# Recurrent heads of a hybrid layer: pairs of different 128-token chunks through carried 128x128 states instead of blocks of a dense 512x512 weight matrix

## The reference, cut to what matters

```python
def hgrn2_chunk_scan(q, k, v, g):
    """Chunkwise S_t = diag(exp g_t) S_{t-1} + k_t v_t^T, o_t = S_t^T q_t.
    q,k,g: (B,S,H,K), v: (B,S,H,V) float32, g = log forget gate. Returns (B,S,H,V)."""
...
    def step(state, inp):
        qc, kc, vc, gc = inp
        b = jnp.cumsum(gc, axis=2)
        diff = b[:, :, :, None, :] - b[:, :, None, :, :]
        decay = jnp.exp(jnp.where(tri[:, :, None], diff, -jnp.inf))
        att = jnp.einsum('bhtk,bhsk,bhtsk->bhts', qc, kc, decay)
        o = (jnp.einsum('bhts,bhsv->bhtv', att, vc)
             + jnp.einsum('bhtk,bhkv->bhtv', qc * jnp.exp(b), state))
        b_last = b[:, :, -1:, :]
        state = (jnp.exp(b_last[:, :, 0, :])[..., None] * state
                 + jnp.einsum('bhsk,bhsv->bhkv', kc * jnp.exp(b_last - b), vc))
        return state, o
```

## Time and profile before

| what | value |
|---|---|
| median of three runs | 3098.46 us (3096.57 to 3101.62) |
| profiled execution, its span | 3093.4 us |
| median less span (what lies around the span) | 5.1 us |
| TensorE busy | 2997.9 us, 97% of the span |
| weight loads busy | 2355.2 us, 76% |
| VectorE busy | 1750.6 us, 57% |
| ScalarE busy | 1000.6 us, 32% |
| GpSimd busy | 1976.8 us, 64% |

### The profile page before, as it was taken

How to read it: one execution, slowest core, us unless ns; L and a number is a source line. 1 busy time by engine, 2 the same in 40 slices (tenths; PEclk the granted TensorE clock), 3 DMA queues, 4 the chain that set the end, 5 groups by cost and what they waited for, 6 DMA issues and landing times.

```text
span 3093.4 us, 39590 instructions
## 1 busy us (share of the span) xinstructions
PE 2997.9 (97%) x15236; PEld 2355.2 (76%) x15236; DVE 1750.6 (57%) x2350; ACT 1000.6 (32%) x1712; POOL 1976.8 (64%) x1860
## 2 busy tenths in 40 slices
PE   8999999999999999999999999999999999899997
PEld 6887777788778878777877777777777777687686
DVE  7745887751374569777217443334788778801412
ACT  6243223330233331334103232233544454411422
POOL 6665676577676656756757655555567777566364
PEclk9999999999999999999999999999999999999998
DMA  5322222233223222222432222222212222232122
GB/s 210 110 102 103 82 93 84 82 142 123 99 106 109 102 86 90 97 82 75 172 109 97 84 86 70 83 72 77 79 69 83 73 80 81 93 133 98 66 89 89
DMA packets 59340, 298.68 MB, mean 97 GB/s; under 512 B 6512, under 2 KB 7408, under 8 KB 29200
## 3 DMA queue, kind: packets, MB, share of 16 engines
q1 hardware_dynamic: 36960, 251.67, 23.1%
q10 hardware_dynamic: 22192, 44.48, 4.2%
HBM read 274.04 MB, written 16.84 MB: 94 GB/s over the span
## 4 chain that ended last, share of the span: by engine, by line
PE 74%; DVE 16%; ACT 4%; POOL 3%; issue 2%; DMA 1%; ACTq 1%; DVEq 0%; POOLq 0%
PE bank L433 65%; POOL w_lo L2595 2%; DVE rec_ex L2432 1%; DVE rec_cum L2297 1%; PE bank L777 1%; POOL w_hi L2593 1%; ACT att_sc L1322 1%; PE bank L786 1%; PE bank L794 1%; DMA w_raw<-in_wall 1%; DVE newton L1796 1%; DVE newton L1798 1%; DVE bank L1899 1%; DVE att_sc L2173 1%; PE bank L966 1%
## 5 line engine op out<-in xcount | busy, mean ns | idle before, releaser
L433 PE MATMUL bank<-h_hi,w_lo 128*128 128x512 f32 x3712 | 1501.6, 405 | 24.7 <-POOL w_lo L2595 14.8
L433 PE MATMUL bank<-h_hi,w_hi 128*128 128x512 f32 x3712 | 1453.0, 391 | 0.0
L433 PE MATMUL bank<-h_lo,w_hi 128*128 128x512 f32 x3712 | 1451.5, 391 | 0.0
L2593 POOL TENSOR_SCALAR w_hi<-w_raw 128x512 fp32r<-128x512 f32 x928 | 705.3, 760 | 1004.0 <-PE bank L433 913.0
L2595 POOL TENSOR_TENSOR w_lo<-w_raw,w_hi 128x512 fp32r<-128x512 f32 x928 | 1294.0, 1394 | 77.4
L433 PEld LDWEIGHTS bank<-h_hi,w_lo 128*128 128x128 f32 x3712 | 700.6, 189 | 230.4 <-issue 52.2
L433 PEld LDWEIGHTS bank<-h_hi,w_hi 128*128 128x128 f32 x3712 | 700.1, 189 | 150.9
L433 PEld LDWEIGHTS bank<-h_lo,w_hi 128*128 128x128 f32 x3712 | 701.7, 189 | 146.2 <-issue 10.5
L1034 ACT ACTIVATE raw<-bank 128x512 f32<-128x512 f32 x148 | 88.5, 598 | 403.9 <-PE bank L433 366.3
L2098 DVE SCALAR_TENSOR_TENSOR bank<-cfm_up,par,bank 128x512 f32<-128x512 f32 x232 | 175.4, 756 | 8.3
L1805 DVE TENSOR_TENSOR sumsq<-sumsq,bank 128x512 f32<-128x512 f32 x80 | 55.0, 688 | 178.8 <-ACT bank L1718 144.7
(11 more groups left out here) (370 smaller groups left out, 2690.8 us busy)
## 6 DMA issues: line engine op xcount, KB each, us to landing
w_raw<-in_wall SPq DMA_DIRECT2D x230, 1024.0 KB, 4.9
x_scratch<-xT ACTq DMA_DIRECT2D x12, 1024.0 KB, 5.0
xT<-x_scratch ACTq DMA_DIRECT2D x12, 1024.0 KB, 8.9
ssd_abc<-acs_scratch ACTq DMA_DIRECT2D x16, 512.0 KB, 3.8
first_xin<-in_x SPq DMA_DIRECT2D x4, 1024.0 KB, 11.2
out<-last_z SPq DMA_DIRECT2D x4, 1024.0 KB, 4.1
w_raw<-in_wall SPq DMA_DIRECT2D x8, 256.0 KB, 10.2
att_tq<-att_uq ACTq DMA_DIRECT2D x32, 64.0 KB
```

What stands on the lines that cost most here:

```text
L433: mm = t.matmul(bank[BANK[u]][:, :], w[:, CS16[k]], h[:, k, :], start=(k == 0 and w is m.w_lo[b]), stop=(k == KT - 1 and w is m.w_hi[b] an ...
L2593: g.tensor_scalar(m.w_hi[b][:, part], m.w_raw[b][:, part], 1.0, 1.0, ALU.mult, ALU.mult).then_inc(*s.hi.inc(u, n))
```

## The change

Only chunks and their own tokens stay in A: `am` becomes 128x4x128, the diagonal blocks alone, and `combine` four matmuls of 128x128. Everything between different chunks goes through states of 128x128 (key width by value width), three for each direction, one for each chunk from which something flows on:

- `keys(j)` on TensorE, in the place of `far(j)`: six transposes of the decayed keys into banks 4 and 5; ScalarE copies them out (`keys`, two copies of 128x384).
- `states(j)` after level 2: six matmuls of 128x128, keys times values, into the same banks.
- `carried(j)` on VectorE, between its levels 3 and 4: two copies and four multiply-adds of 128x128, which carry each state to the next chunk.
- `far(j)` after level 4: six matmuls of 128x128, states times decayed queries `fq`, into bank 6; `combine` then adds to that bank.

VectorE makes the two decayed keys first and the two decayed queries second (into new tiles `fq`); `far_small` is gone; `gather` is one copy of 128x512 from bank 3 after level 1, and stands before `decays(j, 5)`. Head 7 has the same in the same places. The diff, with hunks left out that only repeat this for head 7 or remove a call:

```diff
@@ -52,6 +52,7 @@
 LEVELS = (16, 8, 4, 2, 1, 0)
+FAR_CHUNKS = ((0, 1, 2), (3, 2, 1))
 TWO_PI = 2.0 * math.pi
@@ -369,9 +370,8 @@
         self.lev = t("lev", [P, NLEV])
-        weights = t("weights", [P, NC * (T + P)])
-        self.am = [weights[:, c * T:(c + 1) * T] for c in range(NC)]
-        self.diag = weights[:, :].rearrange("p (c n) -> p c n", n=T + P)
+        self.am, self.keys = t("am", [P, NC, P]), t("keys", [P, 6, P])
+        self.fq = [t(f"fq{d}") for d in range(2)]
         assert m.at >= m.band.end
@@ -826,36 +826,48 @@
             t.wait_ge(*act.at("evac", UNIT["hv", 2, j]))
-            if j:
-                t.wait_ge(*act.at("oT", 3, j - 1))
             for c in range(NC):
...
+        def keys(j):
+            t.wait_ge(*dve.at("fk", j))
+            for d, chunks_of in enumerate(FAR_CHUNKS):
+                for n, c in enumerate(chunks_of):
+                    mm = t.transpose(bank[4 + d][:, CS[n]], q.lk[d][:, CS[c]], m.ident)
+            mm.then_inc(*pe.inc("keys", j))
+
+        def states(j):
+            t.wait_ge(*act.at("keys", j))
+            t.wait_ge(*act.at("vtok", 3, j))
+            for d, chunks_of in enumerate(FAR_CHUNKS):
+                for n, c in enumerate(chunks_of):
+                    mm = t.matmul(bank[4 + d][:, CS[n]], q.keys[:, 3 * d + n, :], q.vtok[:, c, :], start=True, stop=True)
+            mm.then_inc(*pe.inc("states", 3, j))
+
         def far(j):
-            Q = lambda d, c: q.lq[d][:, CS[c]]
-            K = lambda d, c: q.lk[d][:, CS[c]]
-            q2 = q.small
-            pairs = [(0, 1, 0, Q(0, 1)), (0, 2, 0, q2[:, 0, :]), (0, 3, 0, q2[:, 2, :]), (1, 2, 0, Q(0, 2)),
-                     (1, 3, 0, q2[:, 1, :]), (2, 3, 0, Q(0, 3)), (1, 0, 1, Q(1, 0)), (2, 1, 1, Q(1, 1)),
-                     (2, 0, 1, q2[:, 3, :]), (3, 2, 1, Q(1, 2)), (3, 1, 1, q2[:, 4, :]), (3, 0, 1, q2[:, 5, :])]
-            t.wait_ge(*dve.at("fk", j))
-            t.wait_ge(*act.at("q2", j))
-            for src, dst, d, rhs in pairs:
-                mm = t.matmul(bank[3 + src][:, CS[dst]], K(d, src), rhs, start=True, stop=True)
+            t.wait_ge(*dve.at("st", 3, j))
+            if j:
+                t.wait_ge(*act.at("oT", 3, j - 1))
+            for d, chunks_of in enumerate(FAR_CHUNKS):
+                for n, c in enumerate(chunks_of):
+                    to = c + 1 - 2 * d
+                    mm = t.matmul(bank[6][:, CS[to]], q.small[:, 3 * d + n, :], q.fq[d][:, CS[to]], start=(d == 0 and n == 0), stop=False)
             mm.then_inc(*pe.inc("far", j))
...
             t.wait_ge(*dve.at("lev", j, n))
+            if n == 0 and j:
+                t.wait_ge(*act.at("am", j - 1))
             if n == 2:
...
                     for x in range(0, P, 2 * h):
-                        mm = t.matmul(bank[3 + c][x:x + 2 * h, o + x:o + x + 2 * h], q.lk[b][:, o + x:o + x + 2 * h],
+                        mm = t.matmul(bank[3][x:x + 2 * h, o + x:o + x + 2 * h], q.lk[b][:, o + x:o + x + 2 * h],
                                       qq[:, o + x:o + x + 2 * h], start=True, stop=True)
@@ -867,7 +879,7 @@
             for c in range(NC):
-                mm = t.matmul(bank[2][:, :], q.vtok[:, c, :], q.am[c], start=(c == 0), stop=(c == NC - 1))
+                mm = t.matmul(bank[6][:, CS[c]], q.vtok[:, c, :], q.am[:, c, :], start=False, stop=(c == NC - 1))
             mm.then_inc(*pe.inc("o", 3, j))
@@ -885,7 +897,7 @@
                 quarters(us, 0, 4)
-            far(j)
+            keys(j)
             quarters(us, *((4, 5) if j == 0 else (0, 2)))
@@ -895,10 +907,12 @@
             level(j, 2)
+            states(j)
             quarters(us, 6, 8)
...
             level(j, 4)
+            far(j)
             quarters(us, 9, 11)
@@ -1549,14 +1565,14 @@
             a.wait_ge(*act.now())
-            a.activation(chunks(q.ex[1][:, 0, :]), f[:, :, inc], ACT.Exp).then_inc(*act.inc("far0", j))
-            a.wait_ge(*act.now())
             a.activation(q.gx[:, 1, :], q.gx[:, 1, :], ACT.Exp).then_inc(*act.inc("far1", j))
...
             a.wait_ge(*act.now())
+            a.activation(chunks(q.ex[1][:, 1, :]), g[:, :, exc], ACT.Exp).then_inc(*act.inc("far3", j))
+            a.wait_ge(*act.now())
+            a.activation(chunks(q.ex[1][:, 0, :]), f[:, :, inc], ACT.Exp).then_inc(*act.inc("far0", j))
+            a.wait_ge(*act.now())
             a.activation(q.gx[:, 0, :], q.gx[:, 0, :], ACT.Exp).then_inc(*act.inc("far2", j))
-            a.wait_ge(*act.now())
-            a.activation(chunks(q.ex[1][:, 1, :]), g[:, :, exc], ACT.Exp).then_inc(*act.inc("far3", j))
             a.wait_ge(*act.now())
@@ -1564,17 +1580,14 @@
                 a.wait_ge(*act.now())
-                a.activation(q.diag[x:x + 32, :, x:x + 32], q.near[x:x + 32, :].rearrange("p (c n) -> p c n", n=32),
+                a.activation(q.am[x:x + 32, :, x:x + 32], q.near[x:x + 32, :].rearrange("p (c n) -> p c n", n=32),
                              ACT.Copy).then_inc(*act.inc("near", j))
...
-        def far_small(j):
-            Q = lambda d, c: q.lq[d][:, CS[c]]
-            w = [q.g2[:, d, c:c + 1] for d in range(2) for c in range(2)]
-            a.wait_ge(*dve.at("fq", j))
-            for n, (src, f1) in enumerate(((Q(0, 2), w[0]), (Q(0, 3), w[1]), (q.small[:, 1, :], w[0]), (Q(1, 0), w[2]),
-                                           (Q(1, 1), w[3]), (q.small[:, 3, :], w[3]))):
+        def keys(j):
+            a.wait_ge(*pe.at("keys", j))
+            for d in range(2):
                 a.wait_ge(*act.now())
-                a.activation(q.small[:, n, :], src, ACT.Copy, scale=f1).then_inc(*act.inc("q2", j))
+                a.activation(q.keys[:, 3 * d:3 * d + 3, :], chunks(bank[4 + d][:, 0:3 * P]), ACT.Copy).then_inc(*act.inc("keys", j))
...
@@ -1585,15 +1598,14 @@
         def gather(j):
-            a.wait_ge(*pe.at("level", j, 7))
-            for c in range(NC):
-                a.wait_ge(*act.now())
-                a.activation(q.am[c], bank[3 + c][:, :], ACT.Copy).then_inc(*act.inc("am", j))
+            a.wait_ge(*pe.at("level", j, 1))
+            a.wait_ge(*act.now())
+            a.activation(q.am[:, :, :], chunks(bank[3][:, :]), ACT.Copy).then_inc(*act.inc("am", j))
...
             a.wait_ge(*act.now())
-            a.activation(m.y[:, 8 + j, :], bank[2][:, :], ACT.Copy).then_inc(*act.inc("oT", 3, j))
+            a.activation(m.y[:, 8 + j, :], bank[6][:, :], ACT.Copy).then_inc(*act.inc("oT", 3, j))
             if j:
@@ -1625,6 +1637,7 @@
             evac(u1, m.raw[1])
+            gather(j)
             decays(j, 5)
@@ -1634,19 +1647,19 @@
                 rstd_exp(j - 1)
-            gather(j)
             far(j + 1)
             near(j)
-            far_small(j + 1)
             decays(j + 1, 0)
...
         output(6)
+        keys(7)
         decays(7, 1)
...
         decays(7, 3)
+        gather(7)
         a.wait_ge(*pe.at("read", 2, 0))
@@ -2415,10 +2427,12 @@
             kd = q.kd[j % 2]
-            for dst, x, y, name, done in ((q.lq[0], q.ex[1][:, 0, :], q.qs[:, :], "far0", "fq"),
-                                          (q.lq[1], q.gx[:, 0, :], q.qs[:, :], "far2", "fq"),
-                                          (q.lk[0], q.gx[:, 1, :], kd[:, 0, :], "far1", "fk"),
-                                          (q.lk[1], q.ex[1][:, 1, :], kd[:, 1, :], "far3", "fk")):
+            if j:
+                v.wait_ge(*pe.at("far", j - 1))
+            for dst, x, y, name, done in ((q.lk[0], q.gx[:, 1, :], kd[:, 0, :], "far1", "fk"),
+                                          (q.lk[1], q.ex[1][:, 1, :], kd[:, 1, :], "far3", "fk"),
+                                          (q.fq[0], q.ex[1][:, 0, :], q.qs[:, :], "far0", "fq"),
+                                          (q.fq[1], q.gx[:, 0, :], q.qs[:, :], "far2", "fq")):
                 v.wait_ge(*act.at(name, j))
@@ -2435,7 +2449,7 @@
                 decays(j, n + 1)
-            v.wait_ge(*(pe.at("level", j, n - 2) if n >= 2 else pe.at("far", j)))
+            v.wait_ge(*(pe.at("level", j, n - 2) if n >= 2 else pe.at("keys", j)))
             if h:
@@ -2447,6 +2461,19 @@
                 v.tensor_tensor(q.lk[b][:, :], kd[:, 0, :], kd[:, 1, :], ALU.add).then_inc(*dve.inc("lev", j, n))
+
+        def carried(j):
+            v.wait_ge(*pe.at("states", 3, j))
+            v.wait_ge(*act.at("far4", j))
+            for d in range(2):
+                v.wait_ge(*dve.now())
+                v.tensor_copy(q.small[:, 3 * d, :], bank[4 + d][:, 0:P]).then_inc(*dve.inc())
+            for n in range(1, 3):
+                for d in range(2):
+                    c = FAR_CHUNKS[d][n]
+                    v.wait_ge(*dve.now())
+                    v.scalar_tensor_tensor(q.small[:, 3 * d + n, :], q.small[:, 3 * d + n - 1, :], q.g2[:, d, c - 1:c], bank[4 + d][:, CS[n]],
+                                           ALU.mult, ALU.add).then_inc(*dve.inc("st", 3, j))
...
@@ -2490,6 +2517,7 @@
             level(j, 3)
+            carried(j)
```

(7 more changed lines are left out.)

## The result

The changed kernel takes 3122.36 us (median; 3121.19 to 3124.26), the kernel before 3099.05 us on the same chip: ratio 1.0077, interval 1.0065 to 1.0089. It is slower; the forecast was 3122. Its profiled execution takes 3122.63 us, with a span of 3121.3; that of the kernel before has a span of 3093.4.

What follows compares the result with a forecast made beforehand. VectorE and ScalarE were taken to set the stretch before each level 0, TensorE the one after. 18.2 - 4.5 + 8.5 + 1.8 = +24.0 us on the span of 3093.4, plus 5.1, gave 3122 us; range 3107 to 3131.

Steps and rivals of the forecast that it cites:

- B: Stretch from the end of unit hq to the next level 0; VectorE and ScalarE set it, staying at 34.65 us.
- A: Stretch from level 0 to the end of hq, set by TensorE; grows 2.60 us in heads 0 to 6, +18.2.
- Head 0 really gains 4.5 of B: From head 0 to head 1 VectorE has no finish to do, so TensorE's saved work shortens the time: -4.5 us.
- The clock, 5 x 1.7: TensorE's granted clock falls after the 5.05 us pauses before level 0 of heads 2 to 6: +8.5 us.
- `carried` 1.9 us, hidden, 1.6 us of slack: Six VectorE operations between levels 3 and 4 take 1.9 us, ready 1.6 us before TensorE's level 4: no cost.
- The tail, +1.8: In head 7 VectorE is late, so its added 1.9 us push the end back: +1.8 us, bounds -0.8 and +2.
- The 5.1 us: Time between the profiled span and the median, added to the forecast span of 3117.4 to give 3122.5.
- TensorE is the bound: Rival: 1.90 us off every head, 8 x 1.9 = 15, time 3083, if B falls below 30.1; chance 0.08.
- The clock does not fall: Rival: no fall of TensorE's clock behind the pauses, 15.5 us slower in place of 24.0, time 3114; chance 0.10.
- the second rival: B shortens in part, as VectorE's operation times depend on GpSimd; 2.6 to 4 us less per head, 3093 to 3105; chance 0.08.

Runs made afterwards that it cites:

- run 2: Changed kernel with ScalarE's evacuation of unit hv ahead of the decays instead of behind them; 3119.31 us, ratio 1.0078.
- run 1: Changed kernel with VectorE's finish of the head before last put behind level 0 instead of before it; 3107.37 us, ratio 1.0036.
- run 11: Changed kernel with hv's evacuation first and finish's three root-refining VectorE operations left out in heads 0 to 5, for measuring only; 3094.21 us, ratio 0.9996.
- run 8: Changed kernel with hv's evacuation first, plus 18 unused filler matmuls ahead of level 0 in heads 2 to 6; 3115.47 us, ratio 1.0058.
- run 7: Changed kernel with states and far moved behind level 7 and quarter 13, carried into VectorE's gap before the logarithms; 3104.45 us, ratio 1.0023.
- run 3: Changed kernel with both moves: VectorE's finish behind level 0 and hv's evacuation ahead of the decays; 3106.54 us, ratio 1.0033.
- run 9: Changed kernel with finish in VectorE's gap, hv's evacuation first, three root-refining operations omitted in heads 0 to 5, for measuring only; 3085.01 us, ratio 0.9969.
- run 5: Changed kernel with VectorE's finish in its gap while waiting for ScalarE's logarithms, and hv's evacuation first; 3098.40 us, ratio 0.9999.

## Why the prediction was right

**Its mechanism is right. That the total is so close is in part luck: two of its terms missed by almost 4 us each, in opposite directions.**

- *B is VectorE's and stays*: right, 34.6 us, and the pause is 4.97 us in run 2, where it stands in one piece, against 5.05. Runs 1 and 11 show it by shortening B through VectorE alone, run 8 by giving TensorE more to do there at no cost.
- *A grows by 2.60*: right, 2.65 to 2.70 (the heads without a fall in A, 70.2 and 70.3 against 67.5 and 67.65); run 7 takes it back.
- *Head 0 really gains 4.5 of B*: wrong. It gained 2.4 (31.66 against 34.07), and with 4.4 more in A the head got 2.0 longer where -1.9 was forecast. The step that failed is that only VectorE's operands and TensorE's own work end this B. ScalarE's evacuation of hv was a third candidate. Before, it was hidden behind the six microseconds of `combine` and `far` that were taken away. Runs 2 and 11 show it: with the evacuation first this B is 29.5, and the 4.5 are there.
- *The clock, 5 x 1.7*: a fall follows the pauses in five heads, but it cost 5.0 in place of 8.5. The size of one is right (1.65 us in the three that fell in A, 1.6 in run 1, 1.4 by run 8). The count was off: the same ScalarE wait cut the pause in two, and two falls went into B, where they are hidden. A fall of 10.24 us in head 0 (3.41 before, and 3.41 in run 2) cost 2.4 us that were not counted (A of 32.6 against 30.2 in run 2); its pauses at levels 0 and 1 are VectorE's, 3.69 and 2.33 us. So the clock took 7.4 us in all, near the 8.5, but not where it was forecast.
- *`carried` 1.9 us, hidden, 1.6 us of slack*: 2.1 to 2.2 us, hidden, 3.5 of slack. The copies cost 0.29 as in the earlier trace rows, the multiply-adds 0.35, where 0.29 was taken for both. The choice between the copy and the scan was right: by the Trainium skill, in SBUF — State Buffer (Who interferes with whom), an operation with at most one SBUF input, outside the modes that use both ports, keeps clear of GpSimd, and the same 0.61 to 0.62 and 1.50 us for two and four of them stand in runs 3, 7 and 9. The earlier trace rows did not show "GpSimd busy or not": GpSimd was at work during all 16 of those products, which supports the choice without the comparison.
- *The tail, +1.8*: +2.5, with `carried`'s 0.2 more and a wait of 3.71 at level 4 that the count did not have.
- *The profiled execution*: 3.8 us of its 27.9 arose before the changed code. The stage gave 24.1, the sum said 24.0, and the medians differ by 23.3. The 5.1 us taken for what lies around the span are mostly something else: in the runs of the kernel before, an execution is 1.6 to 1.8 us longer than its span, so its profiled execution was some 3.4 us shorter than the median. The sum is unharmed, as it adds a difference to the median.

Of the rivals, "TensorE is the bound" fell by the pauses, and its condition was tried: it asked for a B below 30.1 us. In run 9 TensorE sets B: it is 29.5, and 1.6 to 1.8 us (forecast 1.90) come off each of heads 1 to 5. But they don't come off the whole kernel, as the rival's 8 x 1.9 would have it: head 6 gives back 1.0 and the stretch behind level 0 of head 7 gives back 7.5. "The clock does not fall" holds for the fillers of run 8 and not for the change.

What stays open: why heads alternate between two lengths in run 5; why the unchanged code ahead differs by 3.8 us between executions; what decides whether the clock falls behind a wait, since equal waits of 1.91 us (run 1), 2.44 (run 3) and 1.92 with 2.77 (the changed kernel) brought it in some heads and not, or elsewhere, in others; and what makes VectorE's operations faster or slower. No run took GpSimd's work away to try the second rival's reason.

## What to carry to other kernels

Ask for each stretch which engine ends it, before counting work. Here 1.8 us less for TensorE in each head made the kernel 0.8% slower, since it took 4.5 from the stretch that VectorE sets and put 2.6 into the one that TensorE sets. When a large piece of work goes away, list everything it was hiding: a ScalarE copy behind a wait became visible in every head, and split the pause in two. The cure was in the list of the engine that ends the stretch: moving four VectorE operations into its own gap, with one ScalarE copy moved forward, brought 0.21% without the change, and cutting 4.4 us out of that list brought the changed kernel from 1.0078 to 0.9996.

## What the runs showed of the hardware

- A pause of TensorE between 4.96 and 4.97 us brought 3.41 us at the lower level of the granted clock in five heads of five (run 2), beginning 0.3 to 0.5 us before the pause ended. Pauses of 2.2 and 0.49 us in each head brought none in five (run 7), one of 1.51 none (run 11).
- Between these it is not settled by the pause: 1.91 us alone brought a fall in two of five heads with the same work around it (run 1), 2.44 us in two of five (run 3), and 1.92 and 2.77 us, 6 us apart, a fall behind the second in three heads and behind the first in two (the changed kernel).
- One such fall costs 1.4 to 1.65 us in a stretch that TensorE sets (runs 1, 3 and 8), and nothing in one that it doesn't (heads 1 and 4 of the changed kernel).
- VectorE's products with two SBUF inputs, 128x512 (`rec_lq`, `rec_lk`), took from 0.69 to at least 1.66 us in every run, and a given one changed between runs as its neighbours moved. So work taken out of VectorE's list came back only in part: 3.46 of 4.4 us in run 11.
